# A gate's conditioning is moved from the second mixer into the router of a two-layer decoder step

## The chip, the core and the metric

The kernel runs on one core of a Trainium2 chip. What is measured is the time of one execution on the device, in microseconds (us). All times in this document that are points in time count from the first instruction of the profiled execution.

## What is computed

One inference step of a two-layer decoder for 256 prompt tokens and 8 samples of 8 tokens, 320 tokens of width 1024 in all. Each of nine conditioning vectors (one for the prompt, eight for the samples) gives six vectors for each layer: shift, scale and gate of the mixer, and shift, scale and gate of the feed-forward part. Cut to what matters here:

```
def adaln_params(c, w, b):
    mod = jax.nn.silu(c) @ w + b
    return jnp.split(mod[:, None, :], 6, axis=-1)
...
        sh1, sc1, gt1, sh2, sc2, gt2 = adaln_params(c, ada_w[l], ada_b[l])
        h = modulate(x, norm1_g[l], sh1, sc1)
        z = h @ w_in[l]
...
        ya, v = chunk_sgu(u, v_raw, v_norm_g[l], v_norm_b[l], sgu_w[l], sgu_b[l], chunk)
        yb, new_buf = pool_mix(buf, p, pos, pool_w[l], pool_scale[l])
        mix = jnp.concatenate([rmsnorm(ya, branch_a_g[l]), rmsnorm(yb, branch_b_g[l])], axis=-1) @ w_out[l]
        x = x + gt1 * mix
        h = modulate(x, norm2_g[l], sh2, sc2)
        if l % 2 == 0:
            f = swiglu(h, ffn_w1[l // 2], ffn_w3[l // 2], ffn_w2[l // 2])
        else:
            f = moe_swiglu(h, router_w[l // 2], moe_w1[l // 2], moe_w3[l // 2], moe_w2[l // 2])
        x = x + gt2 * f
```

Layer 0 has a dense feed-forward part, layer 1 a router that picks two of eight experts for each token. The vector `gt2` of layer 1 is used only when the experts' outputs are added to x, at the very end.

## The kernel before

**Units and the ring.** Every weight is read in units of 1 MB (a block of 128 partitions x 4 x 512 floats). SP issues the loads, in the order of the program, into a ring `raw` of six buffers; the load of a unit waits until the unit six places earlier has been used. There are two kinds of units. A split unit (a projection's or an expert's weights) is copied by ACT into `w_hi` with fewer bits, and DVE computes `w_lo = raw - w_hi`; there are three buffers of each. PE then does three products for each tile (high x high, high x low, low x high). The buffer in the ring is free when DVE has written `w_lo` (semaphore `lo_ready`). A plain unit (a part of `ada_w`, the conditioning) is used by PE straight from the ring, with nine rows of `cT`, in four products with 512 columns each; it is free when PE has used it (`plain_used`).

**Conditioning.** The units of the conditioning come in groups (`GROUPS`). PE collects a group's products in one bank of PSUM (`ROW_BANK`), ACT copies the bank (`modrow`, function `ada_rows`), PE transposes it (`ada_tr`), and DVE adds the bias into `mod` (`ada_add`). Group 6, `SELF_A[1]`, is gate 1 and shift 2 of layer 1, and group 7, `SELF_B[1]`, is scale 2 and gate 2 of layer 1. Each has eight units.

**The second mixer** (`project_in_next`, `mixer(1)`, `project_out(1)`) is layer 1's. Its input projection has six split units j = 0 to 5 (the pooling branch p, then v, then u, two units each), with units of group 6 around the first two, and units of group 7 ahead of j = 3, inside the wait ahead of j = 4, ahead of j = 5, and ahead of the gating products. Unit j is multiplied only when its `w_lo` is there. DVE's order is: the low halves of j = 0 to 2, the pooling arithmetic (`pooled`), the low halves of j = 3 and 4, the statistics of v, the low half of j = 5, the norm of v. ACT copies the pooling products (`yb_copy`) and, when the v units are done, evicts v through a gelu. Four units of the output projection follow; in the last of them PE also begins to transpose x for the router.

**The router.** DVE makes the normalised and modulated token rows `htok` by multiplying the transposed x by rows of scale and adding rows of shift, and the layer's output needs rows of gate 2. These rows are written to DRAM from `mrow` by one DMA (`mod_rows`), and read back by DMAs that broadcast them over partitions: for each kind of row one of 128 partitions for the prompt and eight of 8 partitions for the samples. All of these DMAs stand in SP's queue, among the loads of weights. DVE's `rows_half(0)` waits for them (`rows_in`); it stands in DVE's order ahead of the residual of the second half of x, and PE's last transposes and the router's logits need that residual. While DVE ranks the tokens, PE does filler products that nobody reads (`keep_busy`).

**The experts.** Eight or more items of up to 128 tokens, each with 42 split units (`load_item`, `e_item`). Item 0's tokens are sorted out of `htok` by products, the others are fetched from DRAM by POOL. Item 0 is written out step by step, since the router's tables are made between its steps (`find_places`, `extra_items`, `token_gates`, `sort_places`).

## Time and profile before

| what | value |
|---|---|
| median of 3 runs | 1538.72 us (1538.46 to 1540.65) |
| the profiled execution: its own time | 1538.31 us |
| the profiled execution: span of its instructions | 1536.2 us |
| PE, DVE, ACT, POOL busy | 99%, 77%, 62%, 6% of the span |
| the second mixer and the router in the span | from about 441 to 567 us |
| the items | from 567 us on |

The span runs from the first to the last instruction of the core, and 2.1 us of the execution's time lie outside it. The clock of PE that the throttle grants is shown as a share of 2.4 GHz. Lines named L are lines of the kernel before.

### The profile page before, as it was taken

The numbers are of one execution on the slowest core, as the hardware profiler recorded it, in microseconds if no ns is written. First come the engines' busy times: TensorE is split into PE (matmuls) and PEld (weight loads), VectorE is DVE, ScalarE is ACT, GpSimd is POOL, SyncE is SP. The second block draws the span as 40 slices with busy tenths as digits, with TensorE's granted clock in tenths as the row PEclk, the third lists the DMA queues.
The fourth block names the chain that finished last, engine by engine and source line by source line (L and its number), as shares of the span: only waits on it lengthen the run. The fifth ranks groups of instructions, "written<-read, shape, count | busy, mean of one in ns | idle before, by whom it ended". The sixth has DMA issues, their size and how long they took to land.

```text
span 1536.2 us, 22018 instructions
## 1 busy us (share of the span) xinstructions
PE 1516.6 (99%) x8217; PEld 1291.4 (84%) x8217; DVE 1186.2 (77%) x971; ACT 945.7 (62%) x723; POOL 94.8 (6%) x133
## 2 busy tenths in 40 slices
PE   8999999999999999999999999999999999999997
PEld 6787999999977888888888888888888888888885
DVE  4686445444576869888898888888888888889997
ACT  3454433332444567777777777777777777778774
POOL 3210000000002023000000000000000000001001
PEclk9999999999999999999999999999999999999999
DMA  9998944444457859999999999999999999999993
GB/s 358 388 351 295 350 160 140 141 159 147 153 194 298 253 199 361 353 394 397 369 372 398 379 375 385 381 377 383 381 377 381 383 377 377 384 369 369 400 398 121
DMA packets 235379, 492.61 MB, mean 321 GB/s; under 512 B 10155, under 2 KB 16171, under 8 KB 231226
## 3 DMA queue, kind: packets, MB, share of 16 engines
q1 hardware_dynamic: 227110, 472.82, 83.6%
q0 software_dynamic: 5920, 18.57, 3.2%
q10 hardware_dynamic: 2308, 0.64, 0.2%
q8 instruction: 29, 0.48, 0.1%
q14 instruction: 12, 0.10, 0.0%
HBM read 481.86 MB, written 10.36 MB: 320 GB/s over the span
## 4 chain that ended last, share of the span: by engine, by line
PE 95%; DVE 2%; DMA 1%; ACT 0%; issue 0%; SPq 0%; DVEq 0%; ACTq 0%
PE ps L1791 20%; PE ps L1793 20%; PE ps L1792 20%; PE ps L2228 4%; PE ps L2230 4%; PE ps L2229 4%; PE ps L1819 2%; PE ps L2240 2%; PE ps L2239 2%; PE ps L2238 2%; PE ps L2381 2%; PE ps L2179 1%; PE ps L2180 1%; PE ps L2181 1%; DMA raw<-in_ada_w 1%; PE ps L1942 1%
## 5 line engine op out<-in xcount | busy, mean ns | idle before, releaser
L1144 DVE TENSOR_TENSOR w_lo<-raw,w_hi 128x2048 fp32r<-128x2048 f32 x366 | 835.2, 2291 | 172.5 <-ACT w_hi L767 171.2
L767 ACT ACTIVATE w_hi<-raw 128x2048 fp32r<-128x2048 f32 x366 | 701.7, 1918 | 257.7 <-PE ps L1793 161.1
L1791 PE MATMUL ps<-w_hi,split 128*128 128x512 f32 x1392 | 549.1, 394 | 0.6 <-DVE w_lo L1144 0.5
L1793 PE MATMUL ps<-w_hi,split 128*128 128x512 f32 x1392 | 542.6, 390 | 0.0
L1792 PE MATMUL ps<-w_lo,split 128*128 128x512 f32 x1392 | 542.0, 389 | 0.0
L1791 PEld LDWEIGHTS ps<-w_hi,split 128*128 128x128 f32 x1392 | 261.4, 188 | 58.6 <-DVE w_lo L1144 4.3
L1793 PEld LDWEIGHTS ps<-w_hi,split 128*128 128x128 f32 x1392 | 261.3, 188 | 55.3
L1792 PEld LDWEIGHTS ps<-w_lo,split 128*128 128x128 f32 x1392 | 261.6, 188 | 51.9
L2228 PE MATMUL ps<-split,w_hi 128*128 128x320 f32 x432 | 133.8, 310 | 0.0
L2230 PE MATMUL ps<-split,w_lo 128*128 128x320 f32 x432 | 133.5, 309 | 0.0
L2229 PE MATMUL ps<-split,w_hi 128*128 128x320 f32 x432 | 133.5, 309 | 0.0
L1139 DVE TENSOR_TENSOR w_lo<-raw,w_hi 128x2048 fp32r<-128x2048 f32 x32 | 73.2, 2291 | 41.6 <-ACT w_hi L761 41.6
L761 ACT ACTIVATE w_hi<-raw 128x2048 fp32r<-128x2048 f32 x32 | 61.2, 1912 | 58.9 <-DMA raw<-in_w_in 21.7
L2228 PEld LDWEIGHTS ps<-split,w_hi 128*128 128x128 f32 x432 | 81.1, 188 | 1.7 <-issue 1.7
L2229 PEld LDWEIGHTS ps<-split,w_hi 128*128 128x128 f32 x432 | 81.1, 188 | 0.0
L2230 PEld LDWEIGHTS ps<-split,w_lo 128*128 128x128 f32 x432 | 81.1, 188 | 0.0
L1067 ACT ACTIVATE split<-ps 128x512 fp32r<-128x512 f32 x56 | 33.5, 599 | 64.2 <-PE ps L2381 64.2
L2239 PE MATMUL ps<-split,w_hi 128*128 128x320 f32 x208 | 64.3, 309 | 0.0
L2240 PE MATMUL ps<-split,w_lo 128*128 128x320 f32 x208 | 64.3, 309 | 0.0
L2238 PE MATMUL ps<-split,w_hi 128*128 128x320 f32 x208 | 64.3, 309 | 0.0
L1819 PE MATMUL ps<-raw,cT 128*32 128x512 f32 x384 | 46.7, 598 | 1.0 <-DMA raw<-in_ada_w 0.9
L1496 DVE TENSOR_TENSOR plain<-plain,ps 128x1280 f32<-128x1280 f32 x12 | 17.8, 1487 | 33.0 <-PE ps L2240 33.0
(373 smaller groups left out, 1297.2 us busy)
## 6 DMA issues: line engine op xcount, KB each, us to landing
raw<-in_moe_w SPq DMA_DIRECT2D x336, 1024.0 KB, 7.4
raw<-in_ffn_w SPq DMA_DIRECT2D x42, 1024.0 KB, 5.0
raw<-in_ada_w SPq DMA_DIRECT2D x40, 1024.0 KB, 8.9
raw<-in_w_in SPq DMA_DIRECT2D x12, 1024.0 KB, 9.6
raw<-in_ada_w SPq DMA_DIRECT2D x16, 512.0 KB, 10.9
raw<-in_w_out SPq DMA_DIRECT2D x8, 1024.0 KB, 10.2
item_rows<-plain POOLq DMA_DIRECT2D x12, 512.0 KB, 8.0
plain<-in_x_prompt SPq DMA_DIRECT2D x2, 512.0 KB, 3.8
```

The costliest lines, as they stand in the source:

```text
L767: a.activation(w_hi[:, (s0 + j) % SPL], raw[:, (u0 + j) % RAW], ACT.Copy).then_inc(hi_ready, 1)
L1144: v.tensor_tensor(w_lo[:, (s0 + j) % SPL], raw[:, (u0 + j) % RAW], w_hi[:, (s0 + j) % SPL].bitcast(F32), ALU.subtract).then_inc(lo_ready, 1)
L1791: t_.matmul(out, a_hi, b_hi, start=first_, stop=False)
L1792: t_.matmul(out, a_hi, b_lo, start=False, stop=False)
L1793: return t_.matmul(out, a_lo, b_hi, start=False, stop=last_)
L1819: ins = t_.matmul(ps[QROWS * j:QROWS * (j + 1), ROW_BANK[g], :], cT[:, k, :], raw[:, u % RAW, j, :], start=(i == 0), stop=(i == n_units - 1))
L2228: t_.matmul(out, wh[:, k, mc], h_hi[:, kk, 0:T], start=(kk == 0), stop=False)
L2229: t_.matmul(out, wh[:, k, mc], h_lo[:, kk, 0:T], start=False, stop=False)
L2230: ins = t_.matmul(out, wl[:, k, mc], h_hi[:, kk, 0:T], start=False, stop=(kk == KD - 1))
L2238: t_.matmul(out, wh[:, k, mc], gh[:, k, :], start=(k == 0), stop=False)
L2239: t_.matmul(out, wh[:, k, mc], gl[:, k, :], start=False, stop=False)
L2240: ins = t_.matmul(out, wl[:, k, mc], gh[:, k, :], start=False, stop=(k == KB - 1))
```

## The change

Group 7 is cut in two. The new group 7 is scale 2 alone, four units, of which each now holds 256 rows of `ada_w` and the 1024 columns of one vector. The new group 8, `LAST_GATE`, is gate 2, four units, too.

- In the second mixer one unit of group 7 stands at each place where there were two. One unit of group 6 moves from ahead of the first input unit to the place behind it. The pooling products of j = 3 move from ahead of that unit to behind its first quarter.
- The four units of group 8 are loaded behind the output projection's, ahead of the first expert units. PE uses three of them in the router where the first filler products were and the fourth in place of the last filler, into a bank that is free when ACT has copied the first half of the token rows; ACT makes these copies earlier.
- The first two expert units are loaded ahead of the modulation rows (there were three), and each waits for a later unit than before. The third to the sixth expert units wait for the four of group 8.
- The rows of scale and shift are written and read as before. The rows of gate 2 are transposed by PE in step 4 of item 0, copied by DVE in step 5, and written and read by POOL behind its first fetch, in eleven DMAs.

```
-GROUPS = [(0, 0, 4), (0, 0, 4), (0, 1, 8), (0, 2, 4), (0, 2, 4), (1, 0, 8), (1, 1, 8), (1, 2, 8)]
+GROUPS = [(0, 0, 4), (0, 0, 4), (0, 1, 8), (0, 2, 4), (0, 2, 4), (1, 0, 8), (1, 1, 8), (1, 2, 4), (1, 2, 4)]
-CHUNK = {SELF_B[0]: 4, GATE2: 5}
+LAST_GATE = 8
+CHUNK = {SELF_B[0]: 4, GATE2: 5, SELF_B[1]: 4, LAST_GATE: 5}
...
@@ SP @@
             for j in range(2, N_IN):
                 load_in(1, j)
-                load_ada(SELF_B[1], 2 * j - 4, 2 * j - 2)
+                load_ada(SELF_B[1], j - 2, j - 1)
             for j in range(N_OUT):
                 load_out(1, j)
+            load_ada(LAST_GATE, 0, 4)
...
                 n = i * N_FFN + (S_MOE + j - RAW + 1)
+                if j1 < N_FFN or j0:
+                    if s is None and j < 2:
+                        n = S_MOE - 1 + j
+                    elif s is None and j < 4:
+                        sp.wait_ge(plain_used, n_plain - 4 + j - 1)
                 sp.wait_ge(lo_ready, n if s is None else n + s * 6)
...
+            if j0:
+                sp.wait_ge(plain_used, n_plain)
...
-        sp.wait_ge(plain_used, n_plain)
-        load_item(0, 0, 0, 3)
+        load_item(0, 0, 0, 2)
         sp.wait_ge(rows_cp, 2)
-        sp.dma_start(d['mod_rows'].rearrange("j q c -> q j c"), mrow[0:KD * ROWS]).then_inc(rows_out, 16)
+        sp.dma_start(d['mod_rows'][0:2].rearrange("j q c -> q j c"), mrow[0:KD * ROWS, 0:2]).then_inc(rows_out, 16)
...
-        for j, (wide, narrow) in enumerate(((scale_row, scale_s), (shift_row, shift_s), (gt2p, gt2s[0:NS_TOK]))):
+        for j, (wide, narrow) in enumerate(((scale_row, scale_s), (shift_row, shift_s))):
...
-        load_item(0, 0, 3)
+        load_item(0, 0, 2)
...
@@ POOL, behind its first fetch @@
+        gp.wait_ge(rows_cp, 3)
+        gp.dma_start(d['mod_rows'][2], mrow[0:KD * ROWS, 2]).then_inc(gate_out, 16)
+        gp.wait_ge(gate_out, 16)
+        by_row = d['mod_rows'][2].rearrange("(k r) c -> r k c", r=ROWS)
+        for q in (slice(0, P // 2), slice(P // 2, P)):
+            gp.dma_start(gt2p[q].rearrange("p (k c) -> p k c", c=P),
+                         by_row[0].partition_broadcast(P // 2)).then_inc(gate_in, 16)
+        for b in range(NSEQ):
+            gp.dma_start(gt2s[b * TS:(b + 1) * TS].rearrange("p (k c) -> p k c", c=P),
+                         by_row[1 + b].partition_broadcast(TS)).then_inc(gate_in, 16)
...
@@ ACT @@
         for b in range(NBLK):
+            n = BLK[b]
+            act.wait_ge(xg_done, b + 1)
+            a.activation(x_tok[0:n, b, 0:HALF], ps[0:n, b, :], ACT.Copy).then_inc(xtok_cp, 1)
+        for b in range(NBLK):
             tok_square(b, 1)
...
-            a.activation(x_tok[0:n, b, 0:HALF], ps[0:n, b, :], ACT.Copy)
             a.activation(x_tok[0:n, b, HALF:D], ps[0:n, 4 + b, :], ACT.Copy).then_inc(xtok_cp, 1)
+        ada_rows(LAST_GATE)
...
@@ DVE @@
-            ve.wait_ge(rows_in, 16 * 3 * (1 + NSEQ))
+            ve.wait_ge(rows_in, 16 * 2 * (1 + NSEQ))
...
+                    if s == 2:
+                        ada_add(LAST_GATE)
...
                         sort_places()
+                        ve.wait_ge(rows_tr, 2)
+                        v.tensor_copy(mrow[0:KD * ROWS, 2], ps[0:KD * ROWS, 6, 0:P]).then_inc(rows_cp, 1)
...
@@ PE @@
-            ada(SELF_A[1], 6, 8)
+            ada(SELF_A[1], 5, 8)
...
-                    ada(SELF_B[1], 2 * j - 6, 2 * j - 4)
+                    ada(SELF_B[1], j - 3, j - 2)
...
-                if j == 3:
-                    pe.wait_ge(p_out, 4)
-                    pe.wait_ge(d_done, 2)
-                    pe.wait_ge(layer_in, 128)
-                    for gi in range(3):
-                        mix_pool(1, gi)
...
                 for k in range(KB):
+                    if j == 3 and k == 1:
+                        pe.wait_ge(p_out, 4)
+                        pe.wait_ge(d_done, 2)
+                        pe.wait_ge(layer_in, 128)
+                        for gi in range(3):
+                            mix_pool(1, gi)
                     ins = in_products(1, j, w, k)
...
-            for j in range(3):
+            for j in range(2):
                 t_.transpose(ps[0:KD * ROWS, 6, j * P:(j + 1) * P], mod_cols[j], ident[:])
...
-        ada(SELF_A[1], 2, 6)
+        ada(SELF_A[1], 2, 5)
...
-        keep_busy(RANK_BANK, 3)
+        pe.wait_ge(xtok_cp, NBLK)
+        ada(LAST_GATE, 0, 3)
...
-        keep_busy(LOGIT_BANK, 1)
+        ada(LAST_GATE, 3, 4)
...
+                    if s == 2:
+                        ada_tr(LAST_GATE)
                     if s == 4:
                         item_tokens()
+                        pe.wait_ge(mod_add, LAST_GATE + 1)
+                        t_.transpose(ps[0:KD * ROWS, 6, 0:P], mod_cols[2], ident[:]).then_inc(rows_tr, 1)
```

The order of the instructions shows at three places what moved.

SP's queue before, from the last output unit (`in_w_out`) over the first three expert units (`in_moe_w`) and the modulation rows to the fourth expert unit:

```order
L445 DMA raw<-in_w_out 128x4x512 [waits lo_ready]
L533 DMA raw<-in_moe_w 128x4x512 [waits lo_ready,plain_used]
L533 DMA raw<-in_moe_w 128x4x512 [waits lo_ready] x2
L549 DMA mod_rows<-plain 72x3x128 [waits rows_cp]
L555 DMA split<-mod_rows 128x8x128 [waits rows_out,d_done,pool_mm]
L557 DMA plain<-mod_rows 8x8x128 x8
L555 DMA split<-mod_rows 128x8x128
L557 DMA pp<-mod_rows 8x8x128 x8
L555 DMA sp_<-mod_rows 128x8x128
L557 DMA plain<-mod_rows 8x8x128 x8
L533 DMA raw<-in_moe_w 128x4x512 [waits lo_ready]
```

The same place in the change, again from the last output unit on:

```order
L448 DMA raw<-in_w_out 128x4x512 [waits plain_used]
L448 DMA raw<-in_ada_w 128x2x1024 [waits lo_ready]
L448 DMA raw<-in_ada_w 128x2x1024 [waits plain_used]
L448 DMA raw<-in_ada_w 128x2x1024 [waits lo_ready] x2
L542 DMA raw<-in_moe_w 128x4x512 [waits lo_ready] x2
L559 DMA mod_rows<-plain 72x2x128 [waits rows_cp]
L565 DMA split<-mod_rows 128x8x128 [waits rows_out,d_done,pool_mm]
L567 DMA plain<-mod_rows 8x8x128 x8
L565 DMA split<-mod_rows 128x8x128
L567 DMA pp<-mod_rows 8x8x128 x8
L542 DMA raw<-in_moe_w 128x4x512 [waits lo_ready,plain_used] x2
```

Four conditioning units and two expert units with their waits now stand ahead of the write of the modulation rows, where three expert units stood; one of three sets of broadcasts is gone from the queue.

PE before, ahead of the second v unit (j = 3): two conditioning units (`raw,cT`), the pooling products (`plain,mix`), then the first products of the unit:

```order
L1819 MATMUL ps<-raw,cT 32x512 [waits raw_in5,row_out]
L1819 MATMUL ps<-raw,cT 32x512 x3
L1819 MATMUL ps<-raw,cT 32x512 [waits raw_in0]
L1819 MATMUL ps<-raw,cT 32x512 x3
L2096 MATMUL ps<-plain,mix 128x256 [waits layer_in,d_done,p_out]
L2097 MATMUL ps<-plain,mix 128x64
...
L1791 MATMUL ps<-w_hi,split 128x512 [waits lo_ready]
L1792 MATMUL ps<-w_lo,split 128x512
```

PE in the change at the same place:

```order
L1848 MATMUL ps<-raw,cT 32x512 [waits raw_in5,row_out]
L1848 MATMUL ps<-raw,cT 32x512 x3
L1820 MATMUL ps<-w_hi,split 128x512 [waits lo_ready]
L1821 MATMUL ps<-w_lo,split 128x512
...
L2125 MATMUL ps<-plain,mix 128x256 [waits layer_in,d_done,p_out]
L2126 MATMUL ps<-plain,mix 128x64
```

The unit's first products, with their wait for the low half, have moved ahead of the pooling products, and one conditioning unit is gone.

PE before in the router, from the filler products (`x,ident`, 320 columns) over the ranks to the first product of the token sort:

```order
L2325 MATMUL ps<-x,ident 128x320 [waits s_cp]
L2325 MATMUL ps<-x,ident 128x320 x2
L2332 MATMUL ps<-upto,ones 128x32 [waits chosen_r]
L2333 MATMUL ps<-plain,below 128x16
L2334 MATMUL ps<-plain,below 128x8
L2335 MATMUL ps<-plain,ones 128x8
L2325 MATMUL ps<-x,ident 128x320
L2344 MATMUL ps<-hf,plain 128x128 [waits tok_cp,oh0_ready]
```

PE in the change there, from the first unit of the gate on:

```order
L1848 MATMUL ps<-raw,cT 32x512 [waits row_out,raw_in4,xtok_cp,s_cp]
L1848 MATMUL ps<-raw,cT 32x512 x3
L1848 MATMUL ps<-raw,cT 32x512 [waits raw_in5]
L1848 MATMUL ps<-raw,cT 32x512 x3
L1848 MATMUL ps<-raw,cT 32x512 [waits raw_in0]
L1848 MATMUL ps<-raw,cT 32x512 x3
L2357 MATMUL ps<-upto,ones 128x32 [waits chosen_r]
L2358 MATMUL ps<-plain,below 128x16
L2359 MATMUL ps<-plain,below 128x8
L2360 MATMUL ps<-plain,ones 128x8
L1848 MATMUL ps<-raw,cT 32x512 [waits raw_in1]
```

Conditioning units have taken the places of the fillers.

## Rows read from the trace of the kernel before

**Rows 1.** The page, part 1: busy time of each engine, share of the span, instructions.

```profile
PE 1516.6 (99%) x8217; PEld 1291.4 (84%) x8217; DVE 1186.2 (77%) x971; ACT 945.7 (62%) x723; POOL 94.8 (6%) x133
```

**Rows 2.** Busy times by window in the experts; last: PE clock, DMA share, GB/s.

```profile
800.00:900.00 100.00, 100.00 (x456) 82.79 (x455) 88.23 (x51) 75.04 (x49) 1.73 (x3) 1.00 1.02 383
```

**Rows 3.** The chain of waits through the second mixer: start us, us, what.

```profile
448.97 1.07 PE ps L1819 x8
...
474.98 1.85 PE ps L1819 x16
...
477.41 0.67 PE ps L2096 x2
...
479.57 0.50 PE ps L1791
...
488.03 0.44 PE ps L2082 x4
...
508.32 1.85 PE ps L1819 x16
...
515.52 0.34 PE ps L2179
```

**Rows 4.** Timeline of ACT and DVE in the second mixer: start us, us, instruction.

```profile
447.82 0.74 ACT L835 ACTIVATE split<-hf 128x640 fp32r<-128x640 f32 x1
...
489.89 0.52 ACT L851 ACTIVATE hf<-ps,vec 128x320 f32<-128x320 f32 x1
...
508.36 1.24 ACT L922 ACTIVATE plain<-ps 128x1280 f32<-128x1280 f32 x1 [3.19 <-PE ps L1932]
...
477.23 2.28 DVE L1139 TENSOR_TENSOR w_lo<-raw,w_hi 128x2048 fp32r<-128x2048 f32 x1
```

**Rows 5.** Timeline of SP: expert units, modulation rows, broadcasts.

```profile
510.24 1.47 SPq L533 DMA_DIRECT2D raw<-in_moe_w  x3
515.11 0.33 SPq L549 DMA_DIRECT2D mod_rows<-plain  x1
523.40 0.37 SPq L555 DMA_DIRECT2D split<-mod_rows  x1
...
527.19 2.91 SPq L557 DMA_DIRECT2D pp<-mod_rows  x8
```

**Rows 6.** Timeline of DVE behind the second mixer.

```profile
530.78 2.27 DVE L1139 TENSOR_TENSOR w_lo<-raw,w_hi 128x2048 fp32r<-128x2048 f32 x1
...
543.86 1.42 DVE L1449 TENSOR_TENSOR plain<-ps,split 128x512 f32<-128x512 f32 x2
...
546.06 0.86 DVE L1431 SCALAR_TENSOR_TENSOR x<-ps,mod,x 128x256 f32<-128x256 f32 x2
...
549.92 0.88 DVE L1431 SCALAR_TENSOR_TENSOR x<-ps,mod,x 128x256 f32<-128x256 f32 x2 [2.47 <-PE ps L2181]
...
551.02 0.29 DVE L1438 TENSOR_TENSOR x<-x,smp 128x128 f32<-128x128 f32 x1
```

**Rows 7.** Windows of the broadcasts; columns as in rows 2.

```profile
523.40:532.00 8.60, 8.60 (x61) 8.60 (x60) 8.02 (x17) 3.60 (x4) 0.00 (x0) 1.00 0.78 181
532.00:535.00 3.00, 3.00 (x22) 3.00 (x21) 2.06 (x2) 1.92 (x1) 0.00 (x0) 1.00 0.97 165
```

**Rows 8.** Windows of the router; columns as in rows 2, PE first.

```profile
557.50:560.00 2.50, 1.82 (x10) 1.26 (x10) 1.82 (x8) 2.50 (x6) 1.16 (x4) 0.88 0.00 0
560.00:562.50 2.50, 2.50 (x13) 2.50 (x13) 2.50 (x5) 2.48 (x4) 2.18 (x5) 0.50 0.00 0
...
565.00:567.50 2.50, 2.50 (x21) 2.26 (x20) 0.64 (x1) 0.11 (x1) 1.00 (x2) 1.00 0.95 365
```

**Rows 9.** The page, part 6: the dense layer's loads, median us from issue to landing.

```profile
raw<-in_ffn_w SPq DMA_DIRECT2D x42, 1024.0 KB, 5.0
```

**Rows 10.** Timeline of PE in the router.

```profile
554.40 1.88 PE L2325 MATMUL ps<-x,ident 128*128 128x320 f32 x6
557.11 0.41 PE L2332 MATMUL ps<-upto,ones 128*128 128x32 f32 x2 [0.82 <-DVE upto L1586]
```

More of the change, by code:

```diff
@@ L84 @@
                ("ada", 4), ("out", 0, N_OUT)]
-NEXT_MIXER = [("in", 1, 1), ("ada", 6), ("in", 1, 1), ("ada", 2)] + [("in", 1, 1), ("ada", 2)] * 4 + [("out", 1, N_OUT)]
+NEXT_MIXER = [("in", 1, 1), ("ada", 6), ("in", 1, 1), ("ada", 2)] + [("in", 1, 1), ("ada", 1)] * 4 + [("out", 1, N_OUT), ("ada", 4)]
 PARTS = FIRST_MIXER + [("ffn", 0, 2), ("ada", 10), ("ffn", 0, 1), ("ada", 2), ("ffn", 0, N_FFN - 3)] + NEXT_MIXER
@@ L90 @@
 XS_BANK, XS_BANK0, LOGIT_BANK, RANK_BANK, IDX_BANK = (6, 7), (3, 7), 3, 7, 5
-ROW_BANK = [6, 7, 7, 7, 4, 7, 4, 7]
-TURN_BANK = [5, 7, 5, 1, 4, 5, 5, 5]
+ROW_BANK = [6, 7, 7, 7, 4, 7, 4, 7, 1]
+TURN_BANK = [5, 7, 5, 1, 4, 5, 5, 5, 6]
 KIND = []
@@ L357, in write_program @@
     rows_in = sem("rows_in")
+    gate_in = sem("gate_in")
+    gate_out = sem("gate_out")
     xs_scale = sem("xs_scale")
@@ L929, in mixer @@
                 a.activation(s_rows[0:ROWS], ps[0:ROWS, 6, 3 * P:3 * P + E], ACT.Copy).then_inc(rows_cp, 1)
-                a.activation(mrow[0:KD * ROWS], ps[0:KD * ROWS, 6, 0:3 * P].rearrange("p (j c) -> p j c", c=P),
+                a.activation(mrow[0:KD * ROWS, 0:2], ps[0:KD * ROWS, 6, 0:2 * P].rearrange("p (j c) -> p j c", c=P),
                              ACT.Copy).then_inc(rows_cp, 1)
@@ L1672, in early_part @@
                 ve.wait_ge(y_early[b], 16)
-                ve.wait_ge(xtok_cp, NBLK)
+                ve.wait_ge(xtok_cp, 2 * NBLK)
+                ve.wait_ge(gate_in, 16 * (2 + NSEQ))
                 step(v.scalar_tensor_tensor(out=y0[b][0:n], in0=y0[b][0:n], scalar=y_gate[0:n, 0, b:b + 1],
@@ L2067, in project_in_next @@
                     mix_pool(1, 3)
-                    ada(SELF_B[1], 2, 4)
+                    ada(SELF_B[1], 1, 2)
                     pe.wait_ge(st_cp, 2)
@@ L2109, in mixer @@
         def mixer(l):
-            ada(SELF_B[l], 6 if l else 2, 8 if l else 4)
+            ada(SELF_B[l], 3 if l else 2, 4)
             pe.wait_ge(masked, 1)
@@ L2320, in _ @@
         logits(KB + 2, KD).then_inc(log_mm, 1)
-        def keep_busy(bank, n):
-            for _ in range(n):
-                t_.matmul(ps[:, bank, 0:T], ident[:], x[:, 0, 0:T], start=True, stop=True)
         pe.wait_ge(s_cp, 2)
-        keep_busy(RANK_BANK, 3)
+        pe.wait_ge(xtok_cp, NBLK)
+        ada(LAST_GATE, 0, 3)
         pe.wait_ge(chosen_r, 1)
@@ L2412, in e_item @@
                 if first and j == 0:
-                    pe.wait_ge(xtok_cp, NBLK)
+                    pe.wait_ge(xtok_cp, 2 * NBLK)
                 e_up(e_unit(j), j % 2, j // 2)
```

## The prediction

> **What bounds the kernel now.** I read the page first: PE is busy in 99% of the span [rows 1], and in the expert stage every microsecond of PE is taken [rows 2]. So a change pays only where PE waits, or where PE work goes away. Then I read the chain of waits through the second mixer [rows 3], the timelines of ACT and DVE beside it [rows 4], SP's timeline [rows 5], DVE's timeline behind the mixer [rows 6], the DMA rate of that stretch [rows 7], the clock windows of the router [rows 8], one row of the transfer table [rows 9], and PE's timeline in the router [rows 10]. The reader is to see that conditioning units are cheap on PE (two take 1.85 us, so 0.93 each [rows 3]), that the mixer's PE is held at several places by DVE and ACT, and that SP, a single queue in program order, carries both the weights and the modulation rows for the router.
>
> I call the units I0 to I5 (input projection), a0 to a7 and b0 to b7 (conditioning), O0 to O3 (output projection), g0 to g3 (the gate's four, new) and M0, M1, ... (experts).
>
> **Part 1, the second mixer.** Four units leave, 4 x 0.93 = 3.7 us of PE. Place by place:
> - Before I0 one unit less. I0 started at 450.04 (448.97 + 1.07) [rows 3]; its first input was ready at 448.56 (447.82 + 0.74) [rows 4]. So it starts 1.4 us earlier, but the unit comes back one place later: 1.4 - 0.9 = 0.5 us gained.
> - Before I3. Today PE does two units (474.98 + 1.85 = 476.83), waits 0.58 us for the pooled values, does the pooling products from 477.41 until 479.57, and I3's low half has just come (DVE, 477.23 + 2.28 = 479.51) [rows 3, 4]. The change puts I3's first quarter ahead of the pooling products, but on DVE that low half still stands behind the pooling arithmetic. PE will be there at about 475.4 and wait until 479.0 (479.51 less the 0.5 gained): 3.6 us, in which the pooling products (477.41 to 479.57, 2.16 us), today done inside this wait, are no longer. The unit takes 488.03 - 479.57 = 8.46 us, so it ends at 479.0 + 8.46 + 2.16 = 489.6 instead of 488.03: 1.6 us late.
> - Before I4 the other unit that leaves frees nothing: PE waits there for ACT, whose last copy ends at 489.89 + 0.52 = 490.41 [rows 4] and is triggered by I3's end. Still 1.6 late.
> - Before I5 0.93 us comes off: 0.7 late. After I5 another 0.93, but the gating products need ACT's eviction, which ended at 509.60 (508.36 + 1.24 [rows 4]) where PE began at 510.17 (508.32 + 1.85 [rows 3]); only some 0.4 us of the 0.93 can be used: 0.3 late. The sum over the chunk's two halves is a second DVE operation ahead of the router's gain (some 0.3 us, partly seen), one transpose fewer gives 0.1 back.
>
> I take **0.4 us late** at the end of the mixer, where 3.7 of PE were taken out. Bounds: 0 (all of the last unit used) to 1.6 (none of the later units used).
>
> **Part 2, the router's rows.** This is the main term. Before, SP issued M0 to M2 from 510.24 on and then, at 515.11, the write of the modulation rows; the broadcasts, which wait for it, began at 523.40, 7.9 us after that issue was over [rows 5], and DVE used them at 543.86 [rows 6]. Now the four g units stand ahead of M0 and M1 in the ring of six buffers, so M0 must wait for O2's low half and M1 for O3's, and the write of the rows stands behind M1. O3's low half ends at 530.78 + 2.27 = 533.05 [rows 6], with part 1 at 533.45. M1's issue takes 0.4, so the write goes out at 533.9, 18.8 us later than before. The wait for it: below, 5.0 us (one lone 1 MB load [rows 9], which it stands behind); above, the 7.9 of today with three loads ahead. I take 5.9, nearer to the lone load: 539.8. Two sets of broadcasts remain of three. They are 1.57 MB (2 x 128 x 4 KB and 2 x 64 x 4 KB), and the window of 8.6 us from 523.40 moved 1.56 MB at 181 GB/s [rows 7], so today the second set is through at about 532.0. Below, issuing alone takes 6.7 us (527.19 + 2.91 - 523.40 [rows 5]); above, 9.5 at the lower rate of the second window [rows 7]. I take 8.6 and 0.4 for the last semaphore: 548.8.
>
> DVE then does the row products (543.86 to 546.06, 2.2 us) and the two residuals of the last half (1.4 each, as from 549.92 to 551.02 + 0.29 [rows 6]). The second residual starts at 548.8 + 2.2 + 1.4 = 552.4 instead of 549.92: 2.5 us late, so **2.1 us beyond part 1**. Today's 2.47 us of DVE idling for PE there [rows 6] is cover, already used up. Behind the waiting DVE stand the residuals, behind them PE's transposes and the router logits: nothing else fills PE. Bounds: 0 (5.0 and 6.7 put the rows in at 546.0) to 5.0 (7.9 and 9.5 put them in at 551.7).
>
> **Part 3, the router.** Three g units take 2.8 us of PE from 554.40 where the next real product starts at 557.11 [rows 10]; they replace filler products that nobody reads. **0.2 us**; the fourth takes the place of one more filler and the wait behind it. Above: at half clock the three take 5.6 us, so 2.9. The three copies of ACT that move ahead are off the chain on both sides, in ACT's idle time before its second set of squares.
>
> **Part 4, item 0.** PE gains four transposes (0.44 us, as the four of the row at 488.03 [rows 3]) and one small one, on a PE without gaps [rows 2]: **0.7 us** with their starts (bounds 0.5 to 1.5, if DVE's two sums and a copy delay a low half). The gate's rows go out from POOL's queue: one write and ten broadcasts, 0.79 MB, nothing waits for them before the last item.
>
> **Part 5, the clock.** In the router the granted clock goes down today: 0.50, the lower level of 1.2 GHz, in a window where PE did 13 products, against 21 in a window at 1.00 [rows 8]. Those 8 products are 1.0 us, and the 0.88 of the window ahead adds some 0.3, 1.3 in all, after a PE wait of 0.82 us and short products [rows 10]. Part 1 makes a wait of 3.6 us before I3, longer than that one. I take one such fall to 1.2 GHz there, **1.3 us** (bounds 0 to 1.6, half of a comparable stretch of pure products).
> The Trainium skill (TensorE: Matmul & The Clock Gate, HAM oscillation — how this bites in real kernels) says that a PE that idles between bursts is throttled again and pays at the start of the next one. The trace agrees in the router [rows 8]; no row shows it in the mixer. With the rule the sum is 1543.0, without it 1541.7.
>
> **Sum.** 0.4 + 2.1 + 0.2 + 0.7 + 1.3 = 4.7 us on the profiled execution's 1538.3: **1543.0**. The median of the runs, 1538.7, lies 0.4 above that execution; 0.2%, about what a measurement of this kernel can tell from no change, is 3.1 us, so "same" ends near 1541.8.
>
> **Rivals.**
> - The rows come in time (part 2 costs nothing, because the write does not take long behind one load): 1538.3 + 2.6 = 1540.9, 1539.6 without the clock's fall. For it: DMA is nearly idle at 533 but for M1. Against: 18 broadcasts at the rate of [rows 7] after a chain of two latencies. From 546.3 on DVE's wait is on the path.
> - PE's time is given back. PE is busy 99% [rows 1] and the 3.7 us leave for a place where it waits. 1538.3 - 3.7 + 0.9 = 1535.5. It decides if I3's low half is there when PE comes, at 475.4; DVE's row at 477.23 [rows 4] speaks against it.
> - The rows are later still (bound of part 2): 1543.0 + 2.9 = 1545.9. It is today's wait and the lower rate, both.
> - Item 0 starves. M2 to M5 can only be fetched when PE has used g0 to g3, at some 558 to 562 (554.40 [rows 10], 0.93 for each, the last behind the ranks, all some 3 us late), where before M2 was issued by 511.7 [rows 5]; and the gate's 0.79 MB of 512-byte pieces runs beside weights whose DMA share is 1.02 [rows 2]. At the 181 GB/s of [rows 7] that is 4 us of DMA work: up to 1547. Against it: ACT takes M2 only after the tokens are sorted, some 10 us after its issue, more than the 5.0 of a lone load [rows 9].
> The Trainium skill (DMA: Bandwidth & Descriptors, Issuing engines are not separate DMA queues) says that transfers of all issuing engines interleave on the same 16, so POOL's queue would save issuing time alone. That rule speaks for this rival.
>
> **How the numbers follow.** The forecast 0.50 (1541.5 to 1545, with or without the clock's fall), rows in time 0.20, later still 0.13, starving 0.08, PE's time given back 0.09. Faster: the last alone, 0.09. Same: rows in time and the 0.07 of the forecast without the fall that end below 1541.8, 0.27. Slower: 0.64. The range 1539.6 to 1547.0 leaves out the faster case and the ends of the late ones, less than 2 in 10.
>
> **What would show it.** Part 1: a PE wait of 3 to 4 us on DVE's low half before I3, the pooling products after that unit's first quarter, clock below 1 behind it. Part 2: SP's write of the rows after 533 and DVE's first row product near 549 instead of 543.86, with PE idle before the last transposes. Part 3: no PE wait over 1 us between logits and ranks. Part 4: no PE wait on weights in item 0. The prediction is wrong if the row products start before 546.5, or if I3 starts without a wait.

## The result, and the profile after

The change made the kernel slower: 1549.16 us (median of 6 runs, 1548.61 to 1549.54) against 1541.1 for the kernel before in runs beside it, a ratio of 1.006 with a 95% interval of 1.005 to 1.007, some 8 to 9 us. The forecast was 1543.0 with a range of 1539.6 to 1547.0: the direction was right, the size was not, and the time lies outside the range. In later runs the kernel before took 1539.6 to 1540.1 (medians of 15 to 29 runs over several chips) and the changed one, run again, 1549.44 (ratio 1.0057, 1.0043 to 1.0071).

The page of the changed kernel, part 1, answers to [rows 1]: PE is busy 4.3 us longer than before, and for 98% of a longer span instead of 99%.

```profile
PE 1520.9 (98%) x8213; PEld 1292.1 (83%) x8213; DVE 1186.5 (77%) x975; ACT 946.7 (61%) x724; POOL 105.6 (7%) x144
```

The timeline of PE ahead of the second v unit answers to the chain of [rows 3]; the bracket is the wait and what ended it:

```profile
476.73 1.07 PE L1848 MATMUL ps<-raw,cT 128*32 128x512 f32 x8
481.40 0.50 PE L1820 MATMUL ps<-w_hi,split 128*128 128x512 f32 x1 [3.60 <-DVE w_lo L1163]
...
483.74 0.63 PE L1821 MATMUL ps<-w_lo,split 128*128 128x512 f32 x1
...
484.59 1.06 PE L2125 MATMUL ps<-plain,mix 128*128 128x256 f32 x2
```

The reader sees the forecast wait of 3.6 us on DVE's low half, the pooling products (L2125) behind the first quarter, and products that take 0.63 us where 0.39 is usual. The windows of that stretch (PE busy first, granted clock third from the right) say why:

```profile
478.00:481.00 3.00, 0.00 (x0) 0.00 (x0) 2.96 (x10) 0.00 (x0) 0.00 (x0) 1.00 0.65 183
481.00:484.00 3.00, 2.60 (x8) 2.10 (x9) 0.35 (x1) 0.00 (x0) 0.00 (x0) 0.73 0.83 286
484.00:487.00 3.00, 3.00 (x14) 2.52 (x13) 0.00 (x0) 0.89 (x2) 0.00 (x0) 0.70 0.61 236
487.00:490.00 3.00, 3.00 (x16) 2.50 (x15) 0.34 (x1) 2.85 (x4) 0.00 (x0) 1.00 0.00 0
```

SP's timeline behind the mixer answers to [rows 5], DVE's to [rows 6]:

```profile
525.54 11.62 SPq L542 DMA_DIRECT2D raw<-in_moe_w  x2
537.20 0.47 SPq L559 DMA_DIRECT2D mod_rows<-plain  x1
542.26 0.37 SPq L565 DMA_DIRECT2D split<-mod_rows  x1
...
546.05 2.91 SPq L567 DMA_DIRECT2D pp<-mod_rows  x8
```

```profile
552.36 1.29 DVE L1473 TENSOR_TENSOR plain<-ps,split 128x512 f32<-128x512 f32 x2 [4.72 <-DMA pp<-mod_rows]
...
555.47 0.87 DVE L1455 SCALAR_TENSOR_TENSOR x<-ps,mod,x 128x256 f32<-128x256 f32 x2
```

The write of the modulation rows goes out at 537.20, and DVE, which before waited for PE at the second residual, now waits 4.72 us for the rows. PE's timeline in the router answers to [rows 10], the windows to [rows 8]:

```profile
555.60 0.66 PE L2152 MATMUL ps<-ident,x 128*128 128x128 f32 x4 [2.02 <-DVE x L1462]
...
557.33 1.82 PE L2152 MATMUL ps<-ident,x 128*128 128x128 f32 x8
...
562.34 5.35 PE L1848 MATMUL ps<-raw,cT 128*32 128x512 f32 x24
567.62 0.44 PE L2357 MATMUL ps<-upto,ones 128*128 128x32 f32 x2
```

```profile
553.50:555.50 2.00, 0.08 (x1) 0.00 (x0) 1.97 (x7) 1.37 (x3) 0.00 (x0) 1.00 0.00 0
...
557.50:560.00 2.50, 2.50 (x13) 1.96 (x12) 1.27 (x3) 2.08 (x8) 0.00 (x0) 0.50 0.00 0
560.00:562.50 2.50, 2.50 (x16) 2.43 (x20) 0.69 (x3) 2.33 (x8) 0.00 (x0) 0.50 0.00 0
562.50:565.00 2.50, 2.50 (x16) 0.53 (x16) 2.29 (x20) 2.50 (x6) 0.00 (x0) 0.50 0.01 3
565.00:567.70 2.70, 2.70 (x17) 0.38 (x9) 0.58 (x1) 0.95 (x2) 0.00 (x0) 0.50 0.73 250
```

PE waits 2.02 us, and then transposes, logits and three gate units run at 1.2 GHz. The three units take 5.35 us, and the ranks, for which DVE had been ready since 564.9, stand behind them. Last, POOL's timeline in item 0, and the longest of three waits of PE for a low half there (0.70, 0.25 and 0.29 us):

```profile
680.62 0.77 POOL L726 DMA_DIRECT2D sp_<-mod_rows  x1 [5.29 <-DMA mod_rows<-plain]
688.95 0.70 POOL L726 DMA_DIRECT2D sp_<-mod_rows  x1 [7.56 <-issue]
689.65 1.74 POOL L729 DMA_DIRECT2D plain<-mod_rows  x3
699.02 2.78 POOL L729 DMA_DIRECT2D plain<-mod_rows  x5 [7.64 <-issue]
...
706.26 0.62 POOL L738 DMA_DIRECT2D item_rows<-plain  x1
```

```profile
712.36 0.50 PE L1820 MATMUL ps<-w_hi,split 128*128 128x512 f32 x1 [0.70 <-DVE w_lo L1168]
```

**Where the time went.** Span by span between the two traces (1547.7 - 1536.2 = 11.5 us): 2.26 lie ahead of the mixer's statistics (442.56 against 440.30), where nothing was changed; 1.44 in the mixer (statistics to the first output product, 76.59 against 75.15); 2.24 from there to the last eight transposes of x (557.33 - 519.15 against 551.39 - 515.45); 3.14 from those to item 0 (at 576.36 and 567.28); 2.42 from item 0 to the end. Without the first term that is 9.2; the medians show some 8 to 9.

### The profile page after: what moved, and what is told of

Its sections match the earlier page's. It is cut to its first block, busy times and chain, and to the rows that moved or that the text cites. A ratio compares the mean times of both kernels' runs of the same rounds, so it can differ in the third digit from the quotient of the medians.

```text
span 1547.7 us, 22022 instructions
## 1 busy us (share of the span) xinstructions
PE 1520.9 (98%) x8213; PEld 1292.1 (83%) x8213; DVE 1186.5 (77%) x975; ACT 946.7 (61%) x724; POOL 105.6 (7%) x144
## 4 chain that ended last, share of the span: by engine, by line
PE 92%; DVE 3%; DMA 2%; ACT 1%; SPq 1%; issue 1%; POOL 0%; ACTq 0%; POOLq 0%; DVEq 0%
PE ps L1820 20%; PE ps L1822 19%; PE ps L1821 19%; PE ps L2257 4%; PE ps L2259 4%; PE ps L2258 4%; PE ps L1848 2%; PE ps L2269 2%; PE ps L2267 2%; PE ps L2268 2%; PE ps L2406 2%; PE ps L2052 1%; DMA raw<-in_moe_w 1%; DMA raw<-in_ada_w 1%; PE ps L1971 1%; DVE w_lo L1168 1%
```

## The experiments

The table holds, for each kernel's trace, differences between rows in us: A, from the statistics' first product to project_out's first; B, from the same point to DVE's row products; W, PE's wait ahead of the transposes of the second half of x (0 where none of 0.2 or more is listed); C, from the first of the last eight transposes to item 0's first product; K, how long the granted clock stays at 0.50 in the router (windows of 0.25 us); D, from item 0 to the end of the span. The ratio is to the kernel before in the same runs.

| kernel | A | B | W | C | K | D | median us | ratio (95%) |
|---|---|---|---|---|---|---|---|---|
| before | 75.15 | 103.56 | 0 | 15.89 | 3.4 | 968.9 | 1541.1 | |
| e1_before | 75.16 | 103.57 | 0 | 17.21 | 10.2 | 968.8 | 1540.53 (one) | |
| after | 76.59 | 109.80 | 2.0 | 19.03 | 10.2 | 971.3 | 1549.16 | 1.006 (1.005 to 1.007) |
| e11_after | 77.47 | 111.28 | 2.6 | 18.63 | 10.2 | 971.5 | 1549.44 | 1.0057 (1.0043 to 1.0071) |
| e2_fill | 77.53 | 111.94 | 0.2 | 15.97 | 3.4 | 969.2 | 1545.82 | 1.0035 (1.0022 to 1.0049) |
| e3_rows | 75.04 | 104.17 | 0 | 14.43 | 0 | 969.0 | 1541.11 | 1.0012 (1.0001 to 1.0024) |
| e4_pool | 73.00 | 106.08 | 1.9 | 18.87 | 10.2 | 970.2 | 1544.65 | 1.0035 (1.0022 to 1.0048) |
| e5_gate | 76.59 | 110.65 | 2.9 | 17.99 | 10.2 | 969.1 | 1547.95 | 1.0057 (1.0044 to 1.007) |
| e6_all | 72.98 | 102.32 | 0 | 16.05 | 3.4 | 969.1 | 1538.71 | 0.9996 (0.9987 to 1.0005) |
| e8_rowspool | 72.99 | 102.25 | 0 | 16.13 | 3.4 | 969.0 | 1540.12 | 0.9997 (0.9988 to 1.0006) |
| e9_lofirst | 71.35 | 100.70 | 0 | 14.44 | 0 | 969.4 | 1536.59 | 0.9984 (0.9976 to 0.9993) |
| e13_two | 71.35 | 100.75 | 0 | 17.57 | 6.8 | 969.6 | 1537.7 | 0.9986 (0.9975 to 0.9996) |
| e10_nounits | 76.60 | 111.35 | 3.6 | 19.69 | 13.7 | 970.1 | 1549.82 | 1.0065 (1.0051 to 1.0078) |
| e14_three | 76.58 | 111.57 | 3.8 | 18.72 | 17.1 | 971.5 | 1549.98 | 1.006 (1.0046 to 1.0074) |
| e12_late | 75.12 | 103.53 | 0 | 14.97 | 3.4 | 969.1 | 1539.27 | 0.9998 (0.9988 to 1.0007) |
| e15_late | 75.29 | 103.69 | 0 | 16.06 | 3.4 | 969.0 | 1539.58 | 0.9998 (0.9989 to 1.0007) |
| e16_late | 75.35 | 106.56 | 0 | 17.28 | 10.2 | 969.0 | 1540.18 | 1.0004 (0.9995 to 1.0014) |

**The kernel before again.**

> The kernel before, unchanged, for a trace on the chip of the next three. The two traces at hand already differ by 2.3 us (442.56 against 440.30) where the second mixer's statistics begin, ahead of anything that the change moves. Theory: that belongs to the chip and the run, so this trace starts its second mixer near 442.5 and its time is about 1541. Rival: it belongs to the change (other loads ahead of the mixer), so this trace starts it at 440.3 and takes 1538.5.

Its mixer begins at 441.40, between the two; it repeats A and B to 0.01. The start differs from trace to trace (440.3 to 443.9 over all of them), so the 2.3 us are no part of the change. What did not repeat is the router: the clock is low for 10.2 us instead of 3.4, and C is 1.3 longer. (The changed kernel run again, e11_after, does not repeat its clock either: behind the wait in the mixer it is low for 6.8 us instead of 3.4, A is 77.47, and PE waits 2.6 us instead of 2.0 in the router.) The windows of e1_before show that no wait of PE led to its fall:

```profile
551.00:554.00 3.00, 3.00 (x28) 2.74 (x26) 1.59 (x5) 1.04 (x3) 0.41 (x1) 1.00 0.54 208
554.00:559.00 5.00, 5.00 (x20) 3.95 (x19) 4.22 (x24) 4.69 (x15) 0.00 (x0) 0.54 0.01 2
```

**PE kept busy in its wait.**

```diff
+        for _ in range(7):
+            t_.matmul(ps[:, LOGIT_BANK, P:P + KD * QROWS], ident[:], cT[:].rearrange("p k r -> p (k r)"),
+                      start=False, stop=False)
         pe.wait_ge(x_new, KD + 3)
```

> The changed kernel with seven products that nobody reads (256 columns, about 0.25 us each) put on PE where it waits 2.02 us for the late residual, ahead of the last transposes. Nothing else moves. Theory (the wait of PE lets the clock fall to 1.2 GHz, and the transposes, logits and gate units behind it pay): the granted clock stays at 1.00 from 557 to 567, the stretch from the last transposes to the ranks (557.33 to 567.62, 10.3 us) shrinks by 4 to 4.6 us; the fall comes back later, in the token sort (1.4 us), as it did before the change; 2.5 to 4.5 us faster than the changed kernel, so 3.5 to 5.5 slower than before. Rival (the clock falls by what PE does there, transposes and products with 8 columns, wait or no wait): no gain, 7.5 to 8 slower than before.

```profile
558.00:562.00 4.00, 4.00 (x36) 3.70 (x36) 2.22 (x6) 1.91 (x7) 0.75 (x2) 1.00 0.00 0
562.00:565.50 3.50, 3.50 (x18) 1.49 (x21) 3.06 (x23) 3.19 (x10) 0.00 (x0) 0.52 0.02 7
```

With the wait filled the transposes and most of the logits run at full clock; it falls at 562, at the last logits, for 3.4 us. C is 15.97, 2.7 to 3.1 below that of the changed kernel's two traces, and the median is 3.3 below. So the wait made the fall early and long; it is not the only thing that makes it. The ten times go with the clock: four executions with a mean granted clock of 0.997 or 0.998 took 1541.4 to 1543.4 us, six with 0.993 to 0.995 took 1545.2 to 1549.0.

**The rows ahead of the expert units.**

```diff
-        load_item(0, 0, 0, 2)
         sp.wait_ge(rows_cp, 2)
...
+        load_item(0, 0, 0, 2)
         load_item(0, 0, 2)
```

> The changed kernel with the write of the modulation rows and its eighteen broadcasts put in SP's queue ahead of the first two expert units, so that the write goes out at about 520.7 instead of 537.2. Theory (the row products at 552.36 wait for nothing but these rows, and PE's wait and the clock's fall follow from them): row products at about 547.6, PE's wait of 2.02 us ahead of the last transposes gone, granted clock 1.00 until the gate's units are done; 1.9 us of lateness and 2 to 4.6 us of slow clock come back, 1.4 of it lost again in the token sort: 3 to 5 us faster than the changed kernel, 3 to 5 slower than before. Rival 1 (something else holds the row products): no change. Rival 2 (the expert units, issued some 13 us later, come late for item 0 and stall it): the row products come early, but item 0 waits and most of the gain is lost.

The write went out at 517.40, B is 104.17, PE's wait is gone and the granted clock is 1.00 through the whole router in this trace:

```profile
550.00:555.00 5.00, 4.99 (x48) 4.57 (x46) 3.13 (x7) 2.51 (x11) 0.41 (x1) 1.00 0.00 0
555.00:560.00 5.00, 4.84 (x40) 1.85 (x40) 4.07 (x28) 4.77 (x9) 0.66 (x3) 1.00 0.55 178
```

The three gate units take 2.78 us there (554.98 to 557.69), and the ranks stand 5.73 us behind the last transposes, as before (557.11 - 551.39 = 5.72): at full clock the units are free. The trace is of the shortest of ten executions (1537.15 us); its mean granted clock is 0.998, and 0.994 to 0.997 in the other nine, so the clock was low for longer in them. By the medians this one order in SP's queue gives back some 7 of the 8 to 9 us.

**The pooling products in their old place.**

```diff
+                if j == 3:
+                    pe.wait_ge(p_out, 4)
+                    pe.wait_ge(d_done, 2)
+                    pe.wait_ge(layer_in, 128)
+                    for gi in range(3):
+                        mix_pool(1, gi)
...
-                    if j == 3 and k == 1:
-                        pe.wait_ge(p_out, 4)
-                        pe.wait_ge(d_done, 2)
-                        pe.wait_ge(layer_in, 128)
-                        for gi in range(3):
-                            mix_pool(1, gi)
```

> The changed kernel with the pooling products of the second mixer back ahead of the fourth input unit (j = 3), as they were before the change; one conditioning unit stays ahead of them. Theory (DVE's low half is late either way, so the pooling products cost nothing inside that wait and 2.16 us outside it, and the shorter wait keeps the clock): PE waits some 1.4 us for the pooled values, the unit starts at the same 481.4 and takes 8.46 us instead of 12.06, its end is 3.6 us earlier, of which 2 to 3 reach the end of the mixer: 5 to 6 us slower than before. Rival (what follows waits for ACT and DVE anyway): 0 to 1 us faster than the changed kernel.

```profile
475.09 1.07 PE L1848 MATMUL ps<-raw,cT 128*32 128x512 f32 x8
477.60 0.67 PE L2125 MATMUL ps<-plain,mix 128*128 128x256 f32 x2 [1.44 <-issue]
...
479.75 0.50 PE L1820 MATMUL ps<-w_hi,split 128*128 128x512 f32 x1
```

The products fit into the wait, the unit starts at the same 38.8 us behind the statistics, and the whole 3.6 us arrive at the end of the mixer: A is 73.00, 2.15 shorter than in the kernel before. So the 3.7 us of PE that the change takes away were worth 2.15; moving the pooling products turned that into 1.44 of loss, 2.04 by the move itself (A is 75.04 in e3_rows, where the clock held in the mixer) and 1.55 by the clock that fell behind the longer wait. The rows still come late, and the router is as slow as in the changed kernel.

**The gate's rows in one piece.** DVE's second sum writes gate 2 row by row, and POOL reads rows of 4 KB:

```diff
+                if g == LAST_GATE:
+                    turned = mod_cols[0].rearrange("p (r h m) -> p h m r", h=2, m=4)
+                v.tensor_tensor(turned, out, rows[:, 1], ALU.add).then_inc(mod_add, 1)
...
-            gp.dma_start(gt2p[q].rearrange("p (k c) -> p k c", c=P),
-                         by_row[0].partition_broadcast(P // 2)).then_inc(gate_in, 16)
+            gp.dma_start(gt2p[q], by_row[0].partition_broadcast(P // 2)).then_inc(gate_in, 16)
```

> The changed kernel with gate 2's rows turned so that each vector lies in one piece in DRAM: POOL's ten broadcasts in item 0 then read 4 KB at a time instead of 512 bytes. Issues, bytes and order are as in the changed kernel. Theory (the small pieces hold up the weights: 326 and 319 GB/s at a DMA share of 1.04 to 1.06 where 408 are usual, and PE waits 1.2 us on low halves at 712 to 731): no such wait is left, the rate stays near 400, 0.5 to 2.5 us faster than the changed kernel (in other runs of its POOL part PE lost 0.1 to 1.3), so 5.5 to 7.5 slower than before. Rival (POOL's late fetch and late item write do it, not the pieces): PE still waits at 712 to 731, no gain.

POOL's timeline of this kernel:

```profile
679.77 1.11 POOL L726 DMA_DIRECT2D sp_<-mod_rows  x2 [5.04 <-DMA mod_rows<-plain]
680.88 4.00 POOL L728 DMA_DIRECT2D plain<-mod_rows  x8
685.89 2.40 POOL L708 DMA_INDIRECT plain<-tok_rows,idx_now  x1 [0.82 <-POOL idx_now L731]
698.72 0.59 POOL L736 DMA_DIRECT2D item_rows<-plain  x1 [10.44 <-ACT plain L1121]
```

The ten broadcasts are issued in 5 us instead of 21, PE waits for no low half in item 0, and D is 2.3 below that of the changed kernel's trace. The rate of the DMA engines still falls to 325 GB/s from 680 to 690, where the broadcasts begin, and is 391 and 406 GB/s in the two stretches of 10 us behind, where the changed kernel has some 330 GB/s for 21 us (681 to 702). In the time it is 1.2 to 1.5 at most, inside the intervals. And D is 969.0 in e3_rows and e8_rowspool with the small pieces too, 970.2 in e4_pool: the loss in item 0 comes and goes from trace to trace (0 to 2.6 us), and why is open. POOL's pauses are not enough for it. They stand in all nine traces with small pieces, 6.5 to 7.8 us each, and in four of these (e2_fill, e3_rows, e8_rowspool, e13_two) PE waits for no low half in item 0. In e3_rows:

```profile
678.50 0.70 POOL L726 DMA_DIRECT2D sp_<-mod_rows  x1 [7.17 <-issue]
687.39 2.77 POOL L729 DMA_DIRECT2D plain<-mod_rows  x5 [6.46 <-issue]
```

**All three, and two of them.**

> The changed kernel with three things mended at once: the rows written and broadcast ahead of the first expert units, the pooling products back ahead of the fourth input unit, and the gate's rows in one piece. Theory (the 3.7 us of PE taken out of the mixer do come back as 2.2 us at its end, 73.0 us from the mixer's first products against 75.15, once the pooling products stand in their old place; the rows are then in time; the gate units cost the router nothing while the clock holds): row products near 102, item 0 at 124 to 125 against 126.98, 0.5 to 2.5 us faster than before. Rival (the router's clock falls all the same, as it does in the kernel before): gate units at half clock take back 1 to 2.6 us: 0 to 2 slower than before.

> The same without the third: rows early and pooling products in their old place, the gate's broadcasts in pieces of 512 bytes as in the changed kernel. Theory: 0.1 to 2.4 us slower than the version with all three, by the weights that come late in item 0. Rival (the pieces cost nothing that the weights' lead does not cover): the same time, within 0.5 us.

A and B are as forecast in both; the clock fell in both routers, for 3.4 us, and the gain that was left cannot be told from the kernel before. The third edit makes no difference that the intervals can tell.

**DVE's low half ahead of the pooling arithmetic.** To the three, this is added:

```diff
-                    if j == 3 and k == 1:
+                    if j == 3 and k == 2:
...
                 src = dst
+                if l and j == 0:
+                    lo_to(S_IN[1] + 4)
```

and the pooling products are inside the unit again, behind its second quarter where the change has them behind the first.

> The version with all three, but with the pooling products inside the fourth input unit as the change has them (behind its second quarter), and with DVE's low half of that unit put ahead of most of the pooling arithmetic, where its source is there (472.3 in the changed kernel). Theory (the change's place for the pooling products is good only if the unit can start without DVE's pooling): PE starts the unit right behind the conditioning unit, at 35.3 us from the mixer's first products instead of 38.8, no wait over 0.5 us there, the mixer ends 1 to 1.5 us earlier than with the products in their old place: 1.5 to 4 us faster than before. Rival (ACT's copies of the pooling products come later and hold the gelu and the u units): no gain over the version with all three, or a loss of up to 1 us.

> The best version so far (rows early, gate rows in one piece, DVE's low half ahead of the pooling arithmetic with the pooling products behind the unit's second quarter) without the second of these: the gate's broadcasts read pieces of 512 bytes again. Theory (the pieces cost nothing that the weights' lead does not cover): as fast as with them in one piece, 2 to 3 us faster than before. Rival: 1 to 2 us slower than with them in one piece, by waits for low halves in item 0.

```profile
477.00 1.06 PE L1851 MATMUL ps<-raw,cT 128*32 128x512 f32 x8
477.99 0.50 PE L1823 MATMUL ps<-w_hi,split 128*128 128x512 f32 x1
```

The unit follows the conditioning unit without a wait, 35.2 us behind the statistics instead of 38.8, and A is 71.35. Both versions beat the kernel before, by 0.16% (0.07 to 0.24) and 0.14% (0.04 to 0.25), some 2.4 us; A alone is 3.8 shorter. The theory held: a place inside the unit is good once DVE's order fits it. DVE's new order with the pooling products in their old place was not run, so the two edits are not told apart.

**Fillers in the units' place, twice.**

```diff
-        ada(LAST_GATE, 0, 3)
+        for i in range(3):
+            u = U_OF_PLAIN[GROUP_AT[LAST_GATE] + i]
+            pe.wait_ge(raw_in[u % RAW], 16 * (u // RAW + 1))
+            ins = t_.matmul(ps[:, RANK_BANK, 0:T], ident[:], x[:, 0, 0:T], start=True, stop=True)
+            ins.then_inc(plain_used, 1)
```

> The changed kernel with the first three of the gate's four units left out (gate 2 is then not what it should be); PE does six filler products of 320 columns in their place, as the kernel before did. The rows come as late as in the changed kernel. Theory (the low clock in the router costs what real work PE does there at 1.2 GHz; fillers absorb it): the clock falls as before the last transposes of the changed kernel and for as long (10.2 us), but the ranks start when DVE's counts are there, 2 to 2.6 us earlier behind the last transposes (7.3 to 8 us instead of 9.96), of which up to 1.4 go again in a token sort at the lower clock: item 0 starts 1 to 2.6 us earlier; 5 to 6.5 us slower than before. Rival (the units cost nothing there, the wait and the late rows are all of it): no difference, 7.5 to 8 slower.

> The changed kernel with the first three of the gate's four units left out (gate 2 is then not what it should be), and three filler products in their place, the number that the kernel before had there (1.88 us at full clock; the six of the earlier try were more work than the units). The rows come as late as in the changed kernel. Theory (at half clock the three units are 5.1 to 5.4 us of real work, fillers 3.1 to 3.7): the fall of the clock is as long as with the units (10.2 us or more), the ranks wait for DVE's counts, 7.3 to 8.3 us behind the last transposes instead of 9.95; item 0 starts 1 to 2 us earlier; 5.5 to 7 us slower than before. Rival (the units are no dearer than fillers; late rows and the clock are all): within 0.5 us of the changed kernel.

The first of them had two products where the diff has one, 6.19 us at half clock, and tells nothing of the units. In the second the ranks stand 8.40 us behind the first of the last transposes, against 10.29 and 9.94 in the two traces of the changed kernel, so the units do seem to hold them 1.5 to 1.9 us; but PE waited 3.8 us for the rows in that trace, the clock stayed low until 572.35, and item 0 starts no earlier (C 18.72 against 19.03 and 18.63). The time is that of the changed kernel: the rival stands. With late rows, fillers in the units' place gain nothing that the times show; what the units alone cost at the low clock stays open.

**Late rows in the kernel before, three times.**

```diff
         sp.wait_ge(rows_cp, 2)
+        sp.wait_ge(lo_ready, S_MOE)
         sp.dma_start(d['mod_rows'].rearrange("j q c -> q j c"), mrow[0:KD * ROWS]).then_inc(rows_out, 16)
...
-            ve.wait_ge(rows_in, 16 * 3 * (1 + NSEQ))
+            ve.wait_ge(rows_in, 16 * 2 * (1 + NSEQ))
```

> The kernel before with one edit: the modulation rows are written behind the fourth expert unit instead of behind the third, which waits until 534 us. Mixer, router and item 0 are as before, and all three sets of broadcasts are behind the write. Theory (late rows alone make PE wait in the router, whatever stands in the mixer, and the fall of the clock there costs little where only fillers stand): write at about 534.5, row products 5.9 to 9 us later than the 543.9 of before, the second residual 3 to 6 us late, item 0 as much and up to 1.4 more: 3 to 7 us slower than before. Rival (the router has slack for late rows): under 1 us slower.

> The kernel before with the modulation rows written behind the sixth expert unit, whose load waits for the low half at 533 (the fourth, tried before, did not wait for it: the write went out at 517.4 and the row products did not move), and with DVE's row products waiting for the rows of scale and shift alone, as in the change. Mixer, router and item 0 are as before. Theory (late rows alone make PE wait in the router and lengthen the clock's fall): write at about 533.9, row products at 549 instead of 543.9, second residual 2 to 2.5 us late, PE waits 2 to 2.5 us ahead of the last transposes, and the fall costs 1 to 2.5 us more than the 1.5 of the trace of before: 3 to 5 us slower than before. Rival (fillers absorb the fall): 2 to 2.5 us slower, the lateness alone.

> The kernel before with one wait added in SP's queue: the modulation rows are written when the last output unit's low half is there (533), as in the change, and DVE's row products wait for the rows of scale and shift alone. (The sixth expert unit of the last try stands in a later part of the queue, so the write went out at 517.4 again and nothing moved.) Mixer, fillers and item 0 are as before. Theory (late rows alone make PE wait in the router and lengthen the fall of the clock): write at 533.2, 5.1 us of wait, 10.1 us of broadcasts, row products at 548.5 to 549 instead of 543.9, second residual 2 to 2.5 us late, PE waits as long ahead of the last transposes, the clock is low for 10 us or more instead of 3.4; item 0 starts 3.5 to 6 us later: 3.5 to 6 us slower than before. Rival (with fillers in the gate units' place the fall costs nothing): 2 to 2.5 us slower, the lateness alone.

The first two moved the write behind a fourth unit, whose wait was over at 517.0 and not at 534: the write went out at 517.4, nothing moved. The third is the diff above. Its write goes out at 535.83, and the broadcasts begin 2.0 us later, not 5.1:

```profile
535.83 0.33 SPq L551 DMA_DIRECT2D mod_rows<-plain  x1
537.83 0.37 SPq L557 DMA_DIRECT2D split<-mod_rows  x1
```

The row products are 3.0 us late, which DVE's old idle time of 2.47 takes in ([rows 6]; the second residual is 0.2 late), and the median is that of the kernel before. So my theory for this run fell. It also shows how narrow the cover is: in the changed kernel the write stands right behind a 1 MB load, the reads follow after 5.06 us, and those 3 us more are what goes over the cover. The clock was low for 10.2 us here too, without a wait of PE, as in e1_before, and C is the same to 0.1. The trace is of one of five executions with a mean granted clock of 0.992 or 0.993 (1542.0 to 1543.8 us); six others, at 0.995 to 0.997, took 1538.2 to 1540.2.

## Why the prediction was wrong

**Part 1, the mixer (0.4, and 1.3 for the clock): right.** The wait before I3 was 3.60 us as forecast, the unit contains the pooling products, and the mixer is 1.44 late, against 1.7. The clock's part is not fixed: behind the same 3.6 us wait the granted clock was low for 3.4 us in four of seven traces, 6.8 in two and never in e3_rows, and the unit took 11.9, 12.8 and 10.3 us. Without the fall the mixer is 0.1 early (A 75.04) where 0.4 late was forecast, and the shorter fall costs 1.55 where 1.3 was; which of the three comes is chance, so that the sum came out near 1.7 is in part luck. The rule that the Trainium skill has for it (TensorE: Matmul & The Clock Gate, HAM oscillation — how this bites in real kernels), that a PE idling between bursts is throttled again, fits six of these seven traces. It does not cover the router of the kernel before, where the clock fell in e1_before at 554.40, with PE busy 3.00 of 3.00 us ahead of it.

**Part 2, the rows (2.1): right.** Counted from project_out's start, the row products came 4.8 us later than before (552.36 - 519.15 against 543.86 - 515.45), and the second residual 1.85. PE lost 2.24 up to its last eight transposes: the four ahead of them, which before followed PE's products without a wait, now wait for the first residual of the half. In other traces PE's wait was 1.9 to 3.8 us. From the write to the first broadcast it took 5.06 us, from that to the row products 10.1, where 5.9 and 9.0 were taken.

**Part 3, the router (0.2): the step that failed.** The text priced the gate's units at 2.8 us of full clock in the fillers' place and kept 2.9, the price at half clock, as a bound that never entered the sum or the range. C grew by 3.14. The prediction had put the clock's fall behind PE's wait in the mixer and had forecast PE idle ahead of the last transposes as well, and did not carry the one to the other. In all six traces with that wait left open the clock was low for 10.2 us and more, from 0.2 us behind the first of the last eight transposes or up to 3.8 us ahead of it, and C was 18.0 to 19.7; with the gate's units and the rows in time it was low for 0 to 6.8 and C was 14.4 to 17.6. With the rows late and only the wait filled (e2_fill) C was 15.97. The kernel before has the fall too (3.4 to 10.2 us, C 15.0 to 17.3), but 1.9 to 8.4 us behind the first of the last eight transposes, partly on fillers that nobody waits for. The long fall is not in the traced executions alone: the mean granted clock was 0.991 to 0.993 in the six runs of the changed kernel and 0.993 to 0.997 in 101 runs of the kernel before. How much of the 3.14 the units add to the slow transposes and logits is open (e14_three).

**Part 4, item 0 (0.7): the added work right, a rival put at 0.08 came in.** D is 0.1 to 0.7 longer where PE waits for no low half, and the kernel before has a wait of 0.55 there that the changed ones have not, so the added work is some 0.6 to 1.2 us. The rival that item 0 starves came true in three of five traces with late rows, small pieces and the pooling products inside the unit: PE waits 1.2 to 1.4 us for low halves, and D is 971.3 to 971.5, 2.4 to 2.6 over the kernel before. It was put at 0.08 and by two ways, the units' late fetch and the small pieces. With late rows and 4 KB pieces (e5_gate, one trace) the wait is gone, and with early rows it is gone with either size; POOL's pauses alone do not make it, and what has to come together stays open. The Trainium skill (DMA: Bandwidth & Descriptors, Issuing engines are not separate DMA queues) says that another issuing engine saves sequencer time alone; here SP was spared the 4.0 us that the third set took in its queue before (530.15 to 534.10), and POOL spent 21 us on it.

**The rivals.** That PE's time is given back (1535.5) failed for the reason written, DVE's row at 477.23; with that reason removed (e9_lofirst) the mixer gave back 3.8 us, of which the median shows 2.4.

## What to carry to other kernels

Price a step that is put behind a new wait at the clock that the wait leaves, and ask of every wait that you forecast what it does to the work behind it. A small transfer that others wait for belongs ahead of the large loads in its queue: one order in SP's queue was worth some 7 of the 8 to 9 us here. Work taken out of an engine pays only as far as the next input is there: the same units taken out lost 1.4 us in the mixer, gained 2.15 with the pooling products in their old place, and 3.8 with DVE's low half put first.

## What was not expected of the hardware

A 72-row write was followed by the reads that wait for it after 2.0 us on an idle queue, 5.0 to 5.3 behind one 1 MB load just issued, and 7.0 to 8.3 behind three or four of them. The granted clock fell to 1.2 GHz in the router of the same kernel for 3.4 us in one execution and 10.2 in another, and the stretch from the last transposes to item 0 was 1.3 us longer in the second. POOL's ten broadcasts in 512-byte pieces took 19 to 21 us to issue, with two pauses of 6.5 to 7.8 us that nothing in the profile ends, and 5 us in pieces of 4 KB.
